# Identity matrix added by TensorE in a blocked inverse, its evictions dealt to ScalarE and VectorE in pairs, the next inverse begun a level earlier, and a row spread in rounded parts

## The reference

```python
z = u @ w_in[i]                                   # every head's r, k, v, decay, a, gate; q, k, v of FoX
kk = kk / jnp.maximum(jnp.sqrt(jnp.sum(kk * kk, axis=-1, keepdims=True)), 1e-12)
qh = rmsnorm(heads(q), q_norm); kh = rmsnorm(heads(k), k_norm)
def step(state, inp):                             # RWKV-7, token by token
    sa = einsum(state, -kk_t)
    state = state * w_t + sa[..., None] * (kk_t * a_t) + v_t[..., None] * k_t
    y_t = einsum(state, r_t)
h = h + concat([y_rw, y_fox]) @ w_out[i]
h = h + square(relu(u @ w_ff1[i])) @ w_ff2[i]
```

## Time and profile before

| | |
|---|---|
| median of 3 runs | 2929.39 us (2921.06 to 2933.45) |
| profiled execution | 2923.41 us, span 2921.6 us |
| mean granted TensorE clock | 0.973 of full |
| TensorE busy | 2790.8 us, 96% of the span |
| VectorE, ScalarE, GpSimd busy | 1211.6, 873.1, 190.2 us |
| HBM read and written | 265.82 and 36.31 MB |

### The profile page before, as it was taken

One profiled execution on the slowest core, in us unless ns is written; L12 is line 12 of the kernel. 1 busy time (PEld: TensorE's weight loads), 2 busy tenths in 40 slices (PEclk: granted clock), 3 DMA queues, 4 the chain that ended last, 5 costly groups with the idle time before them and its releaser, 6 DMA issues.

```text
span 2921.6 us, 46323 instructions
## 1 busy us (share of the span) xinstructions
PE 2790.8 (96%) x18012; PEld 2232.7 (76%) x18012; DVE 1211.6 (41%) x1633; ACT 873.1 (30%) x1290; POOL 190.2 (7%) x184
## 2 busy tenths in 40 slices
PE   6999999999877789999999999999999999999997
PEld 4877777777556656888888888888888888888886
DVE  5354445555544443333432344223332234333544
ACT  4334343433333332332222222212222122233323
POOL 3000000000022111110000000000000000011110
PEclk9999999999889988999999999999999999999998
DMA  5444544444331122333333333333333333333333
GB/s 178 130 119 128 153 144 130 115 129 139 105 119 58 40 74 79 94 94 100 93 100 94 97 98 94 100 93 99 95 94 100 93 100 94 96 98 106 96 97 90
DMA packets 529808, 303.41 MB, mean 104 GB/s; under 512 B 56093, under 2 KB 508341, under 8 KB 528701
## 3 DMA queue, kind: packets, MB, share of 16 engines
q1 hardware_dynamic: 481021, 270.05, 32.1%
q10 hardware_dynamic: 43552, 14.71, 1.9%
q0 software_dynamic: 5152, 17.40, 1.5%
HBM read 265.82 MB, written 36.31 MB: 103 GB/s over the span
## 4 chain that ended last, share of the span: by engine, by line
issue 60%; PE 31%; DVE 3%; POOL 2%; DMA 1%; ACT 1%; SPq 0%; POOLq 0%; DVEq 0%; ACTq 0%
PE acc L534 6%; PE acc L535 6%; PE acc L536 6%; PE bank L676 2%; POOL sumsq L1597 2%; PE bank L608 1%; PE bank L595 1%; PE bank L624 1%; PE bank L634 1%; PE acc L676 1%; PE bank L601 1%; PE bank L695 1%; PE bank L686 1%; DVE xx L1422 1%; PE bank L836 0%
## 5 line engine op out<-in xcount | busy, mean ns | idle before, releaser
L1208 DVE TENSOR_TENSOR w_lo<-w_raw,w_hi 128x1024 fp32r<-128x1024 f32 (+1 forms) x422 | 515.9, 1223 | 1307.7 <-ACT w_hi L902 1306.5
L902 ACT ACTIVATE w_hi<-w_raw 128x1024 fp32r<-128x1024 f32 x420 | 445.3, 1060 | 1299.4 <-PE acc L536 1280.4
L534 PE MATMUL acc<-a_hi,w_hi 128*128 128x512 f32 x2080 | 824.7, 396 | 5.1 <-DVE a_lo L1481 5.0
L535 PE MATMUL acc<-a_lo,w_hi 128*128 128x512 f32 x2080 | 815.4, 392 | 0.0
L536 PE MATMUL acc<-a_hi,w_lo 128*128 128x512 f32 x2080 | 815.2, 392 | 0.0
L534 PE MATMUL acc<-b_hi,w_hi 128*128 128x512 f32 x1280 | 498.4, 389 | 0.0
L536 PE MATMUL acc<-b_hi,w_lo 128*128 128x512 f32 x1280 | 497.9, 389 | 0.0
L535 PE MATMUL acc<-b_lo,w_hi 128*128 128x512 f32 x1280 | 497.9, 389 | 0.0
L534 PEld LDWEIGHTS acc<-a_hi,w_hi 128*128 128x128 f32 x2080 | 393.9, 189 | 99.6 <-issue 12.9
L536 PEld LDWEIGHTS acc<-a_hi,w_lo 128*128 128x128 f32 x2080 | 393.8, 189 | 83.6
L535 PEld LDWEIGHTS acc<-a_lo,w_hi 128*128 128x128 f32 x2080 | 393.9, 189 | 82.2 <-issue 1.9
(11 more groups left out here) (249 smaller groups left out, 1927.7 us busy)
## 6 DMA issues: line engine op xcount, KB each, us to landing
w_raw<-in_w_ff SPq DMA_DIRECT2D x256, 512.0 KB, 3.9
w_raw<-in_w_in SPq DMA_DIRECT2D x100, 512.0 KB, 3.8
w_raw<-in_w_out SPq DMA_DIRECT2D x32, 512.0 KB, 3.9
w_raw<-in_w_ple_gate SPq DMA_DIRECT2D x32, 512.0 KB, 3.8
z_d<-ev POOLq DMA_DIRECT2D x50, 256.0 KB, 3.3
ab_d<-ab ACTq DMA_DIRECT2D x8, 1024.0 KB, 6.9
x<-ab_d SPq DMA_DIRECT2D x8, 1024.0 KB, 4.8
xin<-in_x SPq DMA_DIRECT2D x16, 256.0 KB, 2.7
```

Source lines behind the costliest of these rows:

```text
L534: mm(dst, wh, hi[:, kt, :], start=kt == 0, stop=False)
L535: mm(dst, wh, lo[:, kt, :], start=False, stop=False)
L902: A(w_hi[:, s, :, :], w_raw[:, s, :, :], ACT.Copy).then_inc(sg("w_hi_ready"), 1)
L1208: V.tensor_tensor(w_lo[:, s, :, 0:width], w_raw[:, s, :, 0:width], w_hi[:, s, :, 0:width].bitcast(F32), ALU.subtract).then_inc(sg("w_split ...
```

## The change

Four things are changed.

1. **Identity by TensorE.** `first` now starts with 16 products of the identity `eye2` with itself (`identity`) into the banks of P, and P is added on top of them in PSUM. The eviction to `qt` is then a plain copy.
2. **Evictions in pairs.** Of `qt`, X^T, `rr`, `sa` and `y`, group 0 is taken by one engine and group 1 by the other, at the same time: `qt` by VectorE (0) and ScalarE (1), X^T, `rr`, `sa` and `y` by ScalarE (0) and VectorE (1). X stays with ScalarE. Each engine has a semaphore of its own for each (q_ready0, q_ready1 and so on).
3. **Next inverse begun earlier.** The two products that begin the inverse of chunk c + 2 move from `products` to level 5 of the pass before (`start_inverse`), and VectorE's four instructions of `begin` to the end of that pass. The first of the five `nm` is now made by VectorE (`first_level`), the other four by GpSimd.
4. **Row spread by rounded parts.** ScalarE rounds the six rows to `row_hi` (fp32r), VectorE makes `row_lo` by a subtraction from PSUM, and each of the three spreads is two fp32r matmuls, with hi and lo. The matrix of zeros and ones is copied once to fp32r. PE waits for `row_split` in place of `head_rows_ready`.

The core of the diff:

```diff
-                    pe.wait_ge(sg("head_rows_ready"), i + 1)
+                    pe.wait_ge(sg("row_split"), i + 1)
                     for n in range(3):
-                        last = mm(bank[2 + n][:, :], spread[:, n, :], hrt[0:6, :], start=True, stop=True)
+                        mm(bank[2 + n][:, :], spread_r[:, n, :], row_hi[:, :], start=True, stop=False)
+                        last = mm(bank[2 + n][:, :], spread_r[:, n, :], row_lo[:, :], start=False, stop=True)
...
-                                      start=start and (stop or j == 0), stop=stop)
+                                      start=start and (stop or j == 0), stop=stop and (start or j == H - 1))
                 return last
+            def identity(dst, a, b):
+                within(dst, lambda i, m: eye2[i, :], lambda i, m: eye2[i, :], a, b, stop=False)
...
-            def products(c):
+            def start_inverse(c):
                 x = x4[c % NX]
                 pe.wait_ge(sg(f"chunk_landed{c % NX}"), 32 * (c // NX + 1))
-                to_time(p_b, lambda ph, n: x[ph, 2, n, :], lambda ph, n: x[ph, 0:2, n, :], P).then_inc(sg("products_done"), 1)
                 to_time(t_b, lambda ph, n: x[ph, 0, n, :], lambda ph, n: x[ph, 2, n, :])
                 to_time(t_b, lambda ph, n: x[ph, 2, n, :], lambda ph, n: x[ph, 0, n, :], at=H * C, b=TURNED).then_inc(sg("begun"), 1)
+            def products(c):
+                x = x4[c % NX]
+                to_time(p_b, lambda ph, n: x[ph, 2, n, :], lambda ph, n: x[ph, 0:2, n, :], P).then_inc(sg("products_done"), 1)
                 if c > 1:
-                    pe.wait_ge(sg("y_taken"), 2 * (c - 1))
+                    pe.wait_ge(sg("y_taken0"), c - 1)
+                    pe.wait_ge(sg("y_taken1"), c - 1)
...
-                pe.wait_ge(sg("n_ready"), 5 * c + lv)
                 if lv == 1:
+                    pe.wait_ge(sg("products_ready"), 4 * c + 2)
+                    identity(p_b, ROWS, TURNED)
+                    pe.wait_ge(sg("n1_ready"), c + 1)
                     pe.wait_ge(sg("begun_ready"), 2 * c + 2)
                 else:
-                    pe.wait_ge(sg("xt_ready"), 2 * (4 * c + lv - 1))
-                within(p_b, lambda i, m: nm[i, lv - 1, m, :], lambda i, m: xx[i, 0, m, :], ROWS, TURNED).then_inc(sg("pt_done"), 1)
+                    identity(p_b, ROWS, TURNED)
+                    pe.wait_ge(sg("n_ready"), 4 * c + lv - 1)
+                    for g in range(2):
+                        pe.wait_ge(sg(f"xt_ready{g}"), 4 * c + lv - 1)
+                within(p_b, lambda i, m: nm[i, lv - 1, m, :], lambda i, m: xx[i, 0, m, :], ROWS, TURNED, start=False).then_inc(sg("q_done"), 1)
+            def xs_of(lv):
+                return 1 if lv == 0 else 3 - lv % 2
...
             chain = (None, right_side, solve, new_state, output_of_state, output_of_chunk)
+            start_inverse(0)
             for c in range(-1, NC):
                 if c < NC - 1:
                     products(c + 1)
                 for lv in range(1, 6):
                     if c < NC - 1:
                         first(c + 1, lv)
+                    if c < NC - 2 and lv == 5:
+                        start_inverse(c + 2)
                     if c >= 0 and (lv != 3 or c < NC - 1):
...
-                    A(hrt[0:6, :], bank[5][0:6, :], ACT.Copy).then_inc(sg("head_rows_ready"), 1)
+                    A(row_hi[:, :], bank[5][0:6, :], ACT.Copy).then_inc(sg("head_rows_ready"), 1)
...
+            def take_q(c, lv):
+                act.wait_ge(sg("q_done"), 5 * c + lv)
+                A(qt[:, pairs[1], :], low(p_b[1]), ACT.Copy).then_inc(sg("q_ready1"), 1)
             def evict(c, lv):
                 if lv < 5:
                     act.wait_ge(sg("xt_done"), 4 * c + lv)
-                    for g in range(2):
-                        A(xx[:, 0, pairs[g], :], low(t_b[g]), ACT.Copy).then_inc(sg("xt_ready"), 1)
+                    A(xx[:, 0, pairs[0], :], low(t_b[0]), ACT.Copy).then_inc(sg("xt_ready0"), 1)
                 act.wait_ge(sg("x_done"), 5 * c + lv)
                 for g in range(2):
                     if lv < 5:
-                        A(xx[:, 1 + lv % 2, pairs[g], :], low(x_b[g]), ACT.Copy).then_inc(sg("x_ready"), 1)
+                        A(xx[:, 3 - lv % 2, pairs[g], :], low(x_b[g]), ACT.Copy).then_inc(sg("x_ready"), 1)
                     else:
                         A(xf[:, pairs[g], :], low(x_b[g]), ACT.Copy).then_inc(sg("inverse_ready"), 1)
-            def take_sa(c):
-                act.wait_ge(sg("sa_done"), c + 1)
-                for g in range(2):
-                    A(sa[:, pairs[g], :], low(w_b[g]), ACT.Copy).then_inc(sg("sa_ready"), 1)
-            def take_y(c):
-                act.wait_ge(sg("y_multiplied"), c + 1)
-                for q in range(2):
-                    A(y_all[:, q::2, c * C:(c + 1) * C], low(w_b[q]), ACT.Copy).then_inc(sg("y_taken"), 1)
+            def take_chain(c, lv):
+                if lv == 1:
+                    act.wait_ge(sg("r_done"), c + 1)
+                    A(rr[:, pairs[0], :], low(w_b[0]), ACT.Copy).then_inc(sg("r_ready0"), 1)
+                if lv == 2:
+                    act.wait_ge(sg("sa_done"), c + 1)
+                    A(sa[:, pairs[0], :], low(w_b[0]), ACT.Copy).then_inc(sg("sa_ready0"), 1)
...
+                    dve.wait_ge(sg("head_rows_ready"), i + 1)
+                    V.tensor_tensor(row_lo[:, :], bank[5][0:6, :], row_hi[:, :].bitcast(F32), ALU.subtract).then_inc(sg("row_split"), 1)
...
-            def add_ones(c, lv):
-                dve.wait_ge(sg("pt_done"), 5 * c + lv)
-                for g in range(2):
-                    V.tensor_tensor(qt[:, pairs[g], :], low(p_b[g]), eye2[:, None, :].broadcast_to([P, H, C]), ALU.add).then_inc(sg("q_ready"), 1)
-            def take_right_side(c):
-                dve.wait_ge(sg("r_done"), c + 1)
-                for g in range(2):
-                    V.tensor_copy(rr[:, pairs[g], :], low(w_b[g])).then_inc(sg("r_ready"), 1)
+            def first_level(c):
+                dve.wait_ge(sg("products_ready"), 4 * c + 2)
+                V.tensor_tensor(nm[:, 0, :, :], gb[:, c % 2, :, 0, :], const(C_LVL + C, C)[:, None, :].broadcast_to([P, NPAIR, C]), ALU.mult).then_inc(sg("n1_ready"), 1)
+            def take_q(c, lv):
+                dve.wait_ge(sg("q_done"), 5 * c + lv)
+                V.tensor_copy(qt[:, pairs[0], :], low(p_b[0])).then_inc(sg("q_ready0"), 1)
+            def take_xt(c, lv):
+                dve.wait_ge(sg("xt_done"), 4 * c + lv)
+                V.tensor_copy(xx[:, 0, pairs[1], :], low(t_b[1])).then_inc(sg("xt_ready1"), 1)
+            def take_chain(c, lv):
+                if lv == 1:
+                    dve.wait_ge(sg("r_done"), c + 1)
+                    V.tensor_copy(rr[:, pairs[1], :], low(w_b[1])).then_inc(sg("r_ready1"), 1)
+                if lv == 2:
+                    dve.wait_ge(sg("sa_done"), c + 1)
+                    V.tensor_copy(sa[:, pairs[1], :], low(w_b[1])).then_inc(sg("sa_ready1"), 1)
+                if lv == 3 and c < NC - 1:
+                    take_state(c)
+                if lv == 5:
+                    dve.wait_ge(sg("y_multiplied"), c + 1)
+                    V.tensor_copy(y_all[:, 1::2, c * C:(c + 1) * C], low(w_b[1])).then_inc(sg("y_taken1"), 1)
...
             dve.wait_ge(sg("fox_stored"), 16 * NPAIR + 16)
+            begin(0)
             for c in range(-1, NC):
                 if c < NC - 1:
                     masked(c + 1, gb, p_b, 0)
-                    begin(c + 1)
+                    first_level(c + 1)
                     masked(c + 1, gk, x_b, 1)
                 for lv in range(1, 6):
                     if c < NC - 1:
-                        add_ones(c + 1, lv)
-                    if c >= 0 and lv == 1:
-                        take_right_side(c)
-                    if 0 <= c < NC - 1 and lv == 3:
-                        take_state(c)
+                        take_q(c + 1, lv)
+                    if c >= 0 and lv != 3:
+                        take_chain(c, lv)
+                    if c < NC - 1 and lv < 5:
+                        take_xt(c + 1, lv)
+                    if c >= 0 and lv == 3:
+                        take_chain(c, lv)
+                if c < NC - 2:
+                    begin(c + 2)
...
-                for lv in range(1, 6):
+                for lv in range(2, 6):
```

More of the change, by code:

```diff
@@ L194, in build @@
     reset = sb("reset", [P, T], at)
-    spread = sb("spread", [6, 3, P], at)
+    spread_r = sb("spread_r", [6, 3, P], at, F32R)
     wa_in = sb("wa_in", [P, P], at)
@@ L419, in _ @@
                              (reset[:, :], consts[:, C_RESET:C_RESET + T]),
-                             (spread[:, :, :], consts[0:6, C_SPREAD:C_SPREAD + 3 * P].rearrange("p (s n) -> p s n", s=3)),
+                             (hrt[0:6, 0:3 * P].rearrange("p (s n) -> p s n", s=3), consts[0:6, C_SPREAD:C_SPREAD + 3 * P].rearrange("p (s n) -> p s n", s=3)),
```

(13 more changed lines are left out.)

39 lines of the change are left out of this document (24 added, 15 removed).

## The result

The changed kernel takes 2935.63 us in the median of 8 runs (2927.48 to 2940.27), the kernel before 2926.39 in 8 runs beside it (2921.06 to 2933.45): a ratio of 1.0026, 95% interval 1.0015 to 1.0037. A second set of runs gave 1.0021 (1.0007 to 1.0035). So the change costs 6 to 8 us by the ratios, 9 to 10 by the medians. The time is inside the range and inside the 0.5% that was called no change, but its sign is the other one than the forecast of -1 us, and both intervals lie above 1. The profiled execution of after took 2927.48 us, the fastest of its eight, and is 4.1 us above that of before.

A forecast was written before the change was run, and what follows sets the result against it. TensorE was taken to bound the kernel: always busy in the pair stage, stopping for its own code in the chunk stage. A -20 and B +19 gave -1 us, so 2928 from the 2929.4 median; range 2910 to 2946.

The forecast's parts named there:

- A: Pair stage: the spread in rounded fp32r parts gives shorter steps and fewer half-speed stretches; -20 us, bounds -24 and -12.
- B2: Chunk stage: the identity's 1280 more records bring 10 more code fetches at 1.2 us each; +12 us, bounds 0 and +16.
- B1: Chunk stage: the identity's matmuls stand in TensorE's way at 40 levels, 0.47 us each; +19 us.
- B3: Chunk stage: evictions in pairs have `qt` ready 0.34 us sooner, counted 12 times; -4 us, other pairs 0.
- B4: Start of each chunk-stage pass: the early start removes a 1.5 us wait, less 0.5, eight times; -8 us, bounds -12 and 0.
- B: Chunk stage: all changes to the inverse together (identity, its code, evictions in pairs, early start); +19 us, bounds 0 and +33.
- the first (2950): Rival, chunk stage: new fetches cost 1.3 us or more, old hidden ones open; B +33, A -12, 2950 us; chance 0.21.
- The second, hidden fetches: Rival, chunk stage: code fetches are hidden behind the array's work; B2 0, B +5, A -24, 2910 us; chance 0.13.
- The third: Rival, chunk stage: the chain of evictions is the true bound and identities fill waits; B -14, 2895 us; chance 0.04.
- the two named signs of being wrong: The chunk stage coming out shorter than before, or the seven half-speed stretches of the pair stage still being there.

The follow-up runs named there:

- the second kernel with fp32 spreads: The changed kernel with the fp32 spread of before, so the changes to the inverse alone: 2947.96 us, ratio 1.0080 to the kernel before.
- the two-matmul kernel: The changed kernel with each level's identity written by 2 fp32r matmuls over all 128 rows instead of 16: 2899.79 us, ratio 0.9913 to the kernel before.
- the repetition: The changed kernel run again without an edit, for a second profile: 2931.33 us, ratio 1.0021 to the kernel before.

## Why the prediction was wrong

The mechanisms were seen, and the sign of the sum was wrong. Two terms were mis-sized in the same direction, A and B2; B2 also rested on a wrong idea, that code is paid beside the array's work. Part of the miss of B2 was hidden by luck, since the busy time grew less than forecast.

**A, the spread: -20 forecast, -14 to -16 measured.** The shorter step is 1.2 us a pair, not 1.4: the seven distances from 264.75 to 266.65 take 1.90 us, 0.27 each instead of 0.23. Seven are -8.4 for the -9.8 forecast. A stretch costs 1.6, not 1.7. Two were taken to remain in the loop; in the nine profiles with the rounded spread one to three stretches' worth remain, 1.9 in the mean, all behind the sums of squares and none behind one of the 63 rounded spreads. Of the fp32 spreads eleven of 14 are followed by one. From seven to 1.9 is -8, near the -8.5 forecast; from the six of the second kernel with fp32 spreads it is -6.6. The eighth pair gives -1.8 in the mean, for -2: the way from its spread to the stage is 2.4 us shorter, and the subtraction delays the spread by 0.6. Over the nine profiles the stage begins at 812.9 in the mean, 17.5 before that of the kernel before; the -20.4 of the first profile was the largest of the nine. That the medians give another 2 to 3 us less is not explained. It could come from executions of before with fewer than seven stretches. This was read in one profile and is not shown for the others.

In the eighth pair the six matmuls run at half clock, from 770.28, and the added subtraction is waited for, as forecast:

```profile
770.28 0.79 PE L639 MATMUL bank<-row_hi,spread_r 6*128 6x512 f32 x1 [1.39 <-DVE row_lo L1402]
...
772.58 0.62 PE L640 MATMUL bank<-row_lo,spread_r 6*128 6x512 f32 x1
```

**B1, the identity on the array: +19 forecast.** The matmul time as such was right: from the identity at 932.80 to P at 933.32 are 0.52 us, for 0.47. Against the kernel without it the array is busy 15.2 us more, though at a clock of 0.99 against 0.95, so that this is a lower bound. What the step did not see is that this time is not a price of its own. With as many packets it costs nothing, as the two-matmul kernel shows, and one eighth of the columns takes as long.

**B2, its code: +12 forecast, bounds 0 and 16.** This step failed. From before to after the holes grew by 19.9 us (21.0 in the repetition, 23.0 with the inverse alone), above the upper bound. I had set a fetch to the length of a single hole, 1.2 or 1.33 us, and added it to the array's work. The price that counts is that of one packet more in the stage: 2.7 to 3.4 us between kernels that differ by eight or ten, the array's work included. A mean over holes (37.8 us for 53 packets, 0.71) hides it, since a packet's fetch also lies behind the array's work, and small records leave little such work per packet. I had also thought that the old holes would open when the waits go. This is open: from before to the kernel without identity, with 53 packets each, the waits fell by 5.6 us and the holes grew by 2.9, which is within the scatter of the stage.

The Trainium skill, Runtime: NRT & Kernel Launch, Instruction fetch mechanics, has the crossing of a 16 KiB block mostly hidden; by it B2 would be nothing. The runs say otherwise: 31.5 us of stage for ten packets at equal busy time of the array. The measurement decides.

**B3, evictions in pairs: -4 forecast.** The kernel in two matmuls is 3.8 us shorter in the stage than the one without identity, although it does the identity on the array. The waits for `qt` went from 5.9 + 0.9 us before to 2.4 after. It fits, but the stages of two profiles of one kernel differ by 0.7 to 3.2, so it is not measured by itself. That the other pairs give nothing, as I took it, fits the stage of 229.0 us without identity and early start.

**B4, the start of a pass: -8 forecast, -9.2 measured**, with the wait named. The working had a wrong piece: I priced `nm` on VectorE at 1.5 us, so the near hit is in part luck. All instructions of `nm` in after (shortest, median, longest in ns):

```profile
L1685 POOL TENSOR_TENSOR nm<-gb,cst x32: 1254/1270/1792, 817.8 to 1029.2; 128x512 f32<-128x512 f32 x32
L1465 DVE TENSOR_TENSOR nm<-gb,cst x8: 691/692/692, 817.7 to 1024.9; 128x512 f32<-128x512 f32 x8
```

VectorE starts 0.04 us ahead of GpSimd at the same release and is done in 0.69 us each of the eight times. GpSimd's first of each pass takes 1.78 to 1.79 us, its others 1.25 to 1.28. The 1476 of the earlier trace rows was misread. No addition took that long: it is the middle between eight of 0.69 to 1.20 us, the first of each pair, and eight of 1.75. Nor was the one of 694 alone. In the trace of before, GpSimd is at work during all 16. The Trainium skill, SBUF — State Buffer, Who interferes with whom, calls the shared ports an exclusive lock. The trace agrees for `nm`, and shows that it matters who comes first: 0.69 us for VectorE, which comes first, and some 0.5 us more for GpSimd.

**The sum.** B was +22 to +25 in the stage, +23 by the ratio and +26 by the medians, for +19 forecast; A was -14 to -16 for -20. By the ratios that adds up to +8 or +9, where +6 and +8 were measured; by the medians to +11 or +12, where +9 and +10 were. Inside B, from before to after: the busy time grew by 13.1 us for the 19 of B1, the holes by 19.9 for the 12 of B2, and the waits fell by 10.8 for the 12 of B3 and B4. So the errors of B1 and B2 nearly cancel, 33 for 31, and A is the larger part of the miss in the sum. Of the rivals, the first (2950) had the right sign and the right place, but neither its A of -12 nor its B of +33 came. The second, hidden fetches, is refuted by the equal-work comparison. The third is refuted for this kernel: P follows the identity without a wait for an engine, and the stage got longer. But its thought that the identity fills idle time holds for the two-matmul kernel, where the idle time is that of the code. Neither of the two named signs of being wrong came: the stage was longer than before, and the stretches behind the spreads went. They tested the mechanisms and not the sizes.

Against the list of what would show it: 63 packets, 0.27 us for a record of the spread (0.23 forecast), 85.8 us from spread to spread (85.5 forecast), a clock of 0.99 from 180 to 760, 56 holes of 1.0 us in the mean and 1.8 at most, no wait for L1460 at the first P, and 247.5 instead of 243 us of stage.

## What to carry to other kernels

In an unrolled stage of small matmuls count the records before the columns. When "issue" leads TensorE's waits, lay the ends of its holes beside the ends of the code's packets. If they go together, the stage is as long as its code: an added small matmul is paid by its share of a packet, and more columns in a matmul that stands there already are next to free while there are such holes to take them. Write a constant into PSUM with the fewest and widest matmuls that reach it: the same identity cost 28 us in 16 matmuls a level, 6 us in four, and with the gain from the evictions less than nothing in two. And take a price that depends on where clock drops fall from several executions, not from one.

## What was not expected of the hardware

- A matmul of 8 columns takes nearly as long as one of 64: 203 and 225 ns in the mean, 31.6 and 33.1 us busy for 1280 records.
- At equal busy time of TensorE (181.2 us) ten packets of code more made the stage 31.5 us longer. At equal code 15.2 us more of busy time made it no longer.
- TensorE's holes without a named cause end 1.19 to 1.60 us behind the end of a code packet (55 of 56 in after, 38 of 39 before, 37 of 38 with the identity in two matmuls).
- The half-speed stretches of the pair stage are not behind idle time. They stood behind eleven of 14 fp32 spreads with 6 rows, which worked for 2.8 us, and behind none of 63 that took 1.6 us; the others stand behind the sums with 2 columns.
- Of two engines that are released by one event, the one that starts 0.04 us sooner pays nothing (0.69 us), the other 0.5 us (1.79 instead of 1.27).

What stays open: whether the identity of the next level can be laid in a wait. It would have to be written into a bank that other engines read at that time; this was not tried. What sets the 3.25 us between two packets of code is open too.
